# Mixers of three token blocks first, then all feed-forwards, their up projection as seven block products for eight

## What is computed

```python
def trunk(x, ...):
    y, c, g = mixer(rmsnorm(x, norm1[l]), ...)   # w_in, short conv and gated linear attention, w_out
    x = x + y
    y, f = conv_ffn(rmsnorm(x, norm2[l]), ffn_s[l], w_up[l], ffn_conv_w[l], w_down[l])
    x = x + y
    return rmsnorm(x, final_norm), ...

def conv_ffn(xn, prev, w_up, conv_w, w_down):
    u = xn @ w_up                          # 1024 -> 2 * 2816
    uc, new = causal_dwconv(u, prev, conv_w)   # three taps along the tokens
    a, g = jnp.split(uc, 2, axis=-1)
    return (jax.nn.silu(g) * a) @ w_down, new
```

## Time and profile before

| | us |
|---|---|
| median of 3 runs | 2595.28 |
| the profiled execution, from first to last instruction | 2592.0 |
| PE busy | 2487.6 (96%) |
| DVE busy | 1388.8 (54%) |
| ACT busy | 861.8 (33%) |
| POOL busy | 646.4 (25%) |

### The profile page before, as it was taken

How to read it: one execution, slowest core, us unless ns; L and a number is a source line. 1 busy time by engine, 2 the same in 40 slices (tenths; PEclk the granted TensorE clock), 3 DMA queues, 4 the chain that set the end, 5 groups by cost and what they waited for, 6 DMA issues and landing times.

```text
span 2592.0 us, 34435 instructions
## 1 busy us (share of the span) xinstructions
PE 2487.6 (96%) x12744; PEld 2159.8 (83%) x12744; DVE 1388.8 (54%) x2125; ACT 861.8 (33%) x1807; POOL 646.4 (25%) x364
## 2 busy tenths in 40 slices
PE   7999999999999999999999999999999999999996
PEld 7878777788888888887998998798888898898895
DVE  3025556555555555556303446576666666666667
ACT  4332332423332332224622233162332332332333
POOL 2211113233223322223112111322222222222220
PEclk9999999999999999999999999999999999999998
DMA  4111131211111111112411012111111111111101
GB/s 154 58 35 33 35 102 41 74 49 41 49 49 49 42 40 48 49 49 65 151 33 41 25 33 96 35 43 48 40 33 47 40 33 48 40 32 49 40 24 71
DMA packets 154669, 133.77 MB, mean 52 GB/s; under 512 B 5325, under 2 KB 137762, under 8 KB 154594
## 3 DMA queue, kind: packets, MB, share of 16 engines
q1 hardware_dynamic: 154593, 132.72, 16.3%
HBM read 123.69 MB, written 9.01 MB: 51 GB/s over the span
## 4 chain that ended last, share of the span: by engine, by line
PE 72%; issue 12%; DVE 9%; POOL 4%; ACT 3%; DVEq 0%; DMA 0%; ACTq 0%; POOLq 0%; SPq 0%
PE ps L989 23%; PE ps L991 22%; PE ps L990 22%; POOL w_lo L425 3%; DVE resid L1485 3%; POOL hid_lo L668 1%; PE ps L1016 1%; DVE up_a L1502 1%; DVE conv_y L1406 1%; PE ps L1081 1%; DVE x_n L1268 1%; PE ps L1098 1%; PE ps L1102 1%; PE ps L1105 1%; DVE conv_y L1437 1%
## 5 line engine op out<-in xcount | busy, mean ns | idle before, releaser
L989 PE MATMUL ps<-xt_hi,w_hi 128*128 128x512 f32 (+5 forms) x2688 | 947.3, 352 | 8.3 <-DVE xt_lo L1276 7.1
L991 PE MATMUL ps<-xt_lo,w_hi 128*128 128x512 f32 (+5 forms) x2688 | 938.4, 349 | 0.0
L990 PE MATMUL ps<-xt_hi,w_lo 128*128 128x512 f32 (+5 forms) x2688 | 938.3, 349 | 0.0
L425 POOL TENSOR_TENSOR w_lo<-raw,w_hi 128x1024 fp32r<-128x1024 f32 x196 | 489.5, 2504 | 1086.6 <-ACT w_hi L420 1086.6
L989 PEld LDWEIGHTS ps<-xt_hi,w_hi 128*128 128x128 f32 x2688 | 513.7, 191 | 62.7 <-issue 14.1
L990 PEld LDWEIGHTS ps<-xt_hi,w_lo 128*128 128x128 f32 x2688 | 513.8, 191 | 46.9 <-issue 0.2
L991 PEld LDWEIGHTS ps<-xt_lo,w_hi 128*128 128x128 f32 x2688 | 514.4, 191 | 43.2
L1485 DVE TENSOR_TENSOR resid<-resid,ps 128x512 f32<-128x512 f32 x748 | 467.1, 680 | 1.3
L938 ACT ACTIVATE up_u<-ps 128x512 f32<-128x512 f32 (+2 forms) x220 | 112.7, 512 | 666.9 <-PE ps L991 656.0
L989 PE MATMUL ps<-w_hi,hid_hi 128*128 128x512 f32 x704 | 281.8, 400 | 47.0 <-DVE resid L1485 46.1
L991 PE MATMUL ps<-w_lo,hid_hi 128*128 128x512 f32 x704 | 279.8, 397 | 0.0
(11 more groups left out here) (155 smaller groups left out, 2088.5 us busy)
## 6 DMA issues: line engine op xcount, KB each, us to landing
raw<-in_w_up_dram SPq DMA_DIRECT2D x88, 512.0 KB, 3.8
raw<-in_w_in_dram SPq DMA_DIRECT2D x48, 512.0 KB, 3.7
raw<-in_w_down_dram SPq DMA_DIRECT2D x44, 512.0 KB, 4.7
x_in<-in_x_prompt_dram SPq DMA_DIRECT2D x32, 512.0 KB, 4.3
raw<-in_w_out_dram SPq DMA_DIRECT2D x16, 512.0 KB, 3.7
out_dram<-x_n SPq DMA_DIRECT2D x16, 512.0 KB, 2.6
...
```

The costliest lines, as they stand in the source:

```text
L425: pool.tensor_tensor(w_lo[:, s, :], raw[:, s, :], w_hi[:, s, :].bitcast(F32), ALU.subtract).then_inc(lo_ready[s], 1)
L989: pe.matmul(out, lh, rh, start=(first and n == 0), stop=False)
L990: pe.matmul(out, ll, rh, start=False, stop=False)
L991: last = pe.matmul(out, lh, rl, start=False, stop=end)
```

## The change

The token blocks are three: 768, 768, and 512 with the 64 of the running stream (580 columns). First the mixers of all three run, one after the other. Each ends with its second RMSNorm, whose normalised activations are kept as plain fp32 (`xs`); VectorE forms four sums of their quarters (`combine`, halves of the 1024 rows by halves of the columns), and seven operands are stored to DRAM (`x_ops`), as is the residual (`x_mid`). Then the feed-forwards of the three blocks run.

The up projection of a step is now a 2 by 2 by 2 block product in Strassen's manner (Winograd's form): the two halves of the contraction, gate and value half of the weights, and two halves of the token columns (`HALF`, 384 or 290). `up_product` computes seven products of 12 matmuls in place of eight. Its operands are kept in SBUF for a whole block (`xo`, high and low parts); those of the weights are made anew in each step: VectorE sums (`sum_up`, four of 128x512), ScalarE high parts (`high_up`, seven of 128x512), GpSimd low parts (`low_up`, seven of 128x512). VectorE puts the four output quarters together (`r_2`, `r_3`, `put`), and taps, SiLU, product and high and low part of the hidden tile are done once over the whole block of 768 or 578 columns, after the seventh product. The down products of tile f - 2 (`tail`) and f - 1 (`head`) stand between the seven products. The last RMSNorm of a block is done inside steps 0 and 1 of the next one.

The down products, the number of down additions for a token tile and the work of the mixer stages on a token are those of before; weights of the mixer are loaded and split three times in place of two.

The diff, cut to its core:

```diff
-BT = SEQ // 2
-GAP = 2
-NCOL = [BT, BT + GAP + DEC]
-TILES = [BT // P, BT // P + 1]
-CHUNKS = [[(0, 512), (512, 512)], [(0, 364), (364, 364), (728, 362)]]
+NB = 3
+T0 = [0, 768, 1536]
+BTS = [768, 768, 512]
+GAP = 2
+TILES = [6, 6, 5]
+NCOL = [768, 768, 580]
+HALF = [384, 384, 290]
+CHUNKS = [[(0, h), (h, h)] for h in HALF]
+TAIL_SHARE = {12: [2, 2], 10: [2, 1]}
+HEAD_SHARE = {12: [1, 2, 2, 2, 1], 10: [1, 2, 2, 1, 1]}
...
+        x_mid = nc.dram_tensor("x_mid", [SEQ + DEC, D], F32).ap()
+        x_ops = nc.dram_tensor("x_ops", [NB, NP, P, 4, CMAX], F32).ap()
...
     @block.sync
...
+            def load_x_op(b, i):
+                c = HALF[b]
+                sp.dma_start(xo_raw[:, i, 1, :].rearrange("p (k c) -> p k c", k=4)[:, :, 0:c],
+                             x_ops[b, i, :, :, 0:c]).then_inc(xo_loaded[i], 16)
...
+                n2.wait(sp, "hi", 2 * nt)
+                for i, k, c0 in ((0, 0, 0), (2, 4, 0), (6, 4, c)):
+                    sp.dma_start(x_ops[b, i, :, :, 0:c], xs[:, k:k + 4, c0:c0 + c]).then_inc(ops_stored, 16)
+                sp.wait_ge(x_sums, sums_before(b + 1))
+                for i, n in X_SUM.items():
+                    sp.dma_start(x_ops[b, i, :, :, 0:c], tst[:, n, :, 0:c]).then_inc(sums_stored, 16)
...
+                    for t in range(4) if f == 0 else range(4, TILES[b - 1]):
+                        store_result(b - 1, t)
+                        if t < TILES[b]:
+                            load_resid(b, t)
+                if isinstance(f, int) and f == NF - 1 and b + 1 < NB:
+                    for i in range(NP):
+                        sp.wait_ge(up_done, NP * g + i + 1)
+                        load_x_op(b + 1, i)
+                if more:
...
     @block.gpsimd
...
+            def ffn_step(b, f, par, more=True):
+                g = b * NF + f
+                low_up(g, NP - 1)
+                prev = before(b, f, 1)
+                if prev:
+                    pool.wait_ge(h_hi, g)
...
+                                       ALU.subtract).then_inc(h_lo, 1)
+                if isinstance(f, int) and f == 0 and b:
+                    low_x(b, 6)
+                for i in range(NP - 1):
+                    if more:
+                        low_up(g + 1, i)
+                    if i == 1:
+                        pool.wait_ge(wd_high, g + 1)
+                        pool.tensor_tensor(wd_lo[:, par, :], wd_raw[:, :], wd_hi[:, par, :].bitcast(F32), ALU.subtract).then_inc(wd_low, 1)
+                    if isinstance(f, int) and f == NF - 1 and b + 1 < NB and i - 1 in LOW_BY_P:
+                        low_x(b + 1, i - 1)
...
     @block.scalar
...
+            def finish_up(b, f):
+                g = b * NF + f
+                w = tap_cols(b)
+                act.wait_ge(taps_g, 2 * (g + 1))
+                act.activation(up_y[:, 1, 0:w], up_y[:, 1, 0:w], ACT.Silu).then_inc(silu, 1)
+                act.wait_ge(c12_read, g + 1)
+                keep_rows(b, f)
+                wait(act, h_lo, g)
+                taps_start(b, 0, f).then_inc(y_a, 1)
...
+            def ffn_step(b, f, par, more=True):
+                g = b * NF + f
+                h = HALF[b]
+                edge = f if isinstance(f, int) else None
+                prev = before(b, f, 1)
+                if prev:
+                    finish_up(*prev)
+                act.wait_ge(up_done, NP * g + 1)
+                wait(act, c21_read, g)
+                act.activation(r_1[:, 0:h], ps[:, 3 * par, 0:h], ACT.Copy).then_inc(r1_read, 1)
+                act.wait_ge(wu_summed, 4 * g + 4)
+                high_up(g, 6)
+                if edge == 0 and b:
+                    high_x(b, 4)
+                if prev:
+                    high_hidden(*prev, 1 - par)
+                if edge == 0 and b:
+                    high_x(b, 5)
+                    high_x(b, 6)
+                if more:
+                    act.wait_ge(wu_loaded, 32 * (g + 2))
+                    high_up(g + 1, 0)
+                    act.wait_ge(up_done, NP * g + 2)
+                    act.wait_ge(wu_summed, 4 * (g + 1) + S2 + 1)
+                    high_up(g + 1, 1)
+                act.wait_ge(wd_loaded, 16 * (g + 1))
+                if prev:
+                    wait(act, down_done, down_before(*prev))
+                act.activation(wd_hi[:, par, :], wd_raw[:, :], ACT.Copy).then_inc(wd_high, 1)
+                act.wait_ge(up_done, NP * g + 3)
+                wait(act, taps_a, 2 * g)
...
+                wait(act, taps_g, 2 * g)
+                earlier_rows(b, 1, f)
+                act.wait_ge(c21_read, g + 1)
+                wait(act, gated, g)
+                taps_start(b, 1, f).then_inc(y_g, 1)
+                if more:
+                    act.wait_ge(up_done, NP * g + 6)
+                    high_up(g + 1, 5)
+                if edge == NF - 1 and b + 1 < NB:
+                    high_x(b + 1, 2)
+                    high_x(b + 1, 3)
+                if edge in (0, 1) and b:
+                    act.preload_act_table_set("natural_log_exp_and_others")
+                    for t in range(4) if edge == 0 else range(4, TILES[b - 1]):
+                        final_rstd(b - 1, t)
...
     @block.tensor
...
-                            columns(m, (par * 2 * nch + slot) % 4, c0, n).then_inc(ffn.up_done, 1)
-                            if not first_f:
-                                down(f - 1, 1 - par, pair + (par - 1), down_share(b, slot))
+            def up_product(b, par, i):
+                c = HALF[b]
+                bank = {0: 3 * par, 2: 3 * par, 4: 2, 6: 2}.get(i, 1)
+                return product(ps[:, bank, 0:c], [
+                    (wq_hi[:, i, k * P:(k + 1) * P], wq_lo[:, i, k * P:(k + 1) * P],
+                     xo[:, i, 0, k * c_of(k):k * c_of(k) + c], xo[:, i, 1, k * c_of(k):k * c_of(k) + c]) for k in range(4)],
+                    first=i in (0, 1, 4), skip=True)
...
+                    if i == 0:
+                        wait(pe, c11_read, g - 1)
+                    if i == 1:
+                        wait(pe, c21_read, g)
+                    if i == 2:
+                        pe.wait_ge(r1_read, g + 1)
+                    if i == 3:
+                        pe.wait_ge(r2_read, g + 1)
+                    if i == 4:
+                        wait(pe, c12_read, g)
+                    if i == 5:
+                        pe.wait_ge(r3_read, g + 1)
+                    if i == 6:
+                        pe.wait_ge(c22_read, g + 1)
+                    up_product(b, par, i).then_inc(up_done, 1)
+                    if i < 2 and prev2:
+                        down(*prev2, par, tails[i])
+                    if i == 2 and prev:
+                        down_ready(*prev)
+                    if i >= 2 and prev:
+                        down(*prev, 1 - par, heads[i - 2])
...
     @block.vector
...
+                def combine(c0, w):
+                    h = HALF[b]
+                    a, bb = xs[:, 0:4, c0:c0 + w], xs[:, 4:8, c0:c0 + w]
+                    c, d = xs[:, 0:4, h + c0:h + c0 + w], xs[:, 4:8, h + c0:h + c0 + w]
+                    t1, t2, t3, n4 = (tst[:, n, :, c0:c0 + w] for n in range(4))
+                    dve.tensor_tensor(t1, c, a, ALU.subtract).then_inc(x_sums, 1)
+                    dve.tensor_tensor(t3, d, c, ALU.subtract).then_inc(x_sums, 1)
+                    dve.wait_ge(x_sums, done + 1)
+                    dve.tensor_tensor(t2, d, t1, ALU.subtract).then_inc(x_sums, 1)
+                    dve.wait_ge(x_sums, done + 3)
+                    dve.tensor_tensor(n4, bb, t2, ALU.subtract).then_inc(x_sums, 1)
+                    return done + 4
...
+            def sum_up(g):
+                a0, a1, g0, g1 = (wu_raw[:, n, :] for n in range(4))
+                s1, s2, s3, s4 = (wu_sum[:, n, :] for n in range(4))
+                dve.wait_ge(wu_loaded, 32 * (g + 1))
+                wait(dve, wu_lo, NP * g)
+                dve.tensor_tensor(s1, g0, g1, ALU.add).then_inc(wu_summed, 1)
+                dve.wait_ge(wu_summed, 4 * g + 1)
+                dve.tensor_tensor(s2, s1, a0, ALU.subtract).then_inc(wu_summed, 1)
+                dve.tensor_tensor(s3, a0, g0, ALU.subtract).then_inc(wu_summed, 1)
+                dve.wait_ge(wu_summed, 4 * g + 2)
+                dve.tensor_tensor(s4, a1, s2, ALU.subtract).then_inc(wu_summed, 1)
...
+                tail(0)
+                dve.wait_ge(up_done, NP * g + 2)
+                dve.wait_ge(r1_read, g + 1)
+                dve.tensor_tensor(r_2[:, 0:h], ps[:, 1, 0:h], r_1[:, 0:h], ALU.add).then_inc(r2_read, 1)
+                tail(1)
+                if edge == 0 and b:
+                    low_x(b, 5)
+                if more:
+                    sum_up(g + 1)
+                if edge == 1:
+                    dve.wait_ge(resid_ready[0], 16 * 4 * (b + 1))
+                head(2)
+                dve.wait_ge(up_done, NP * g + 4)
```

(26 more changed lines are left out.)

1697 lines of the change are left out of this document (908 added, 789 removed).

## The result

The changed kernel takes 2706.24 us (median of 4 runs, 2705.39 to 2707.3); the kernel before, on the same chip, 2594.57 (2593.25 to 2595.38). The ratio is 1.0432 with a 95% interval of 1.0419 to 1.0445: **4.3% slower**.

The account below looks back on a forecast made before the run. Before: one feed-forward bound by PE, the other also by late VectorE; after: PE waiting for the hidden tile. 1042 + 14 + 1601 + 46 + 31 = 2734, plus 3.3: 2737 us; own range 2690 to 2790, 8 in 10 2550 to 2850.

Parts of the forecast that it names:

- 43 large periods: Steps of the 768-token blocks: period 24.8 us plus 0.5 for the clock, 25.3 each, 1088 together.
- 22 small periods: Steps of the small block: 21.8 us with PE idle 3.9, plus 1.5 for the clock, 23.3 each, 513 together.
- two changes of block: Between feed-forward blocks, operand loads and splits and the last norm hold up ScalarE's SiLU: 23 us each, twice 46.
- PE's own work: Large feed-forward step: 84 matmuls of 384 columns at 0.177 us and 36 of 512 at 0.233, 23.3 us.
- The chain: Large step, sixth product issued to hidden tile's low part: 14.95 us, GpSimd delaying two taps; with PE's 9.86, period 24.8.
- The clock in large blocks: PE waits 1.5 us a period; the clock falls in a third of the steps, 0.5 us a step.
- First step: Start of the feed-forwards: operands pass ScalarE, VectorE and GpSimd at some 2.4 us each, 14.4 for six.
- Mixers: Up to the first up product: 980 now, 5 for narrower chunks, 38 mixer changes, 29 feed-forward start, less 10: 1042 us.
- weights late: Rival, feed-forward steps: single-buffered wu_raw loads come two us late in every step, 2867 us; chance 0.06.
- GpSimd falls into the gaps: Rival, feed-forward steps: both GpSimd subtractions run while VectorE waits for ScalarE, PE never waits, 2554 us; chance 0.25.
- one of the two only: Rival: only one of GpSimd's two subtractions avoids the taps; steps 24.0 and 21.8 us, 2650 us; chance 0.12.
- VectorE becomes the bound: Rival, feed-forward steps: nine VectorE operations each wait 1 us for GpSimd, 27.5 us a large step, 2869 us; chance 0.12.

Follow-up runs that it names:

- the first two runs: Changed kernel with GpSimd's low part of operand 6 moved behind the hidden tile's: 2630.77 us; additionally operand 5's low part made by VectorE: 2602.24 us.
- the run with `r_2` first: Changed kernel with both collisions out, more PE cover for the hidden tile, and r_2 added ahead of the first two down additions on VectorE: 2575.28 us.

## Why the prediction was right, and where it was off

The sign, the mechanism and the place were right, and the time was 31 us too high (2737 against 2706.24), within its own range of 2690 to 2790. Term by term, with the cuts that the prediction had: its first step ends, and its end begins, when PE has issued a sixth product (1053.51 in the first step, 2670.87 in the last).

| term | predicted | measured |
|---|---|---|
| to the first up product | 1042 | 1021.8 |
| first step, to the sixth product issued | 14.4 | 31.7 |
| 43 large periods | 1088 (25.3) | 1037 (24.1) |
| 22 small periods | 513 (23.3) | 525 (23.9) |
| two changes of block (measured: all that steps have over the periods above) | 46 | 55 |
| end | 31 | 33.7 |

The errors partly cancel: mixers 20 and large periods 51 too high, first step 17, small periods 12, changes 9 and end 3 too low. So the total is nearer than its terms, and that is luck.

- **PE's own work** (23.3 us): too high by 0.5. The floor is 22.8. 384 columns take 0.173 us from start to start (twelve from 1304.53 to 1306.61), not the interpolated 0.177, and 512 columns 0.228, not 0.233. By the formula of the Trainium skill that was weighed there ("TensorE: Matmul & The Clock Gate", Back-to-back issue gap) 84 x 0.1625 + 36 x 0.2158 would be 21.4, an estimate; the measured floor is nearer to the interpolation. The page gives that formula for a matmul in isolation and has it too high for a stream of 512 columns; here the stream is slower than the formula, 228 ns against 216.
- **The chain** (14.95 us, period 24.8): right in every link of the large block, 0.8 us too long. With the clock's 0.5 on top the forecast had 25.3 for a measured 24.1. The forecast let a tap wait for GpSimd's whole 1.2 us, it waited 0.8: GpSimd's row begins at 1302.86, while the first tap still runs.
- **The clock in large blocks** (0.5 a step): did not fall at all. With a floor of 22.8 PE loses 1.3 us in each step, and at that the clock held 1.00. In the small block it is idle 3.2 us and the clock fell in every step: 2.1 us, not 1.5.
- **First step** (14.4): 31.7, so 17 us too low, the largest error for its size. I counted six operands at 2.4 us and left out that the result quarters share the same engines: PE waits 3.56 us for ScalarE's `r_1`, which stands behind seven copies of 1.5 us, and 9.37 for VectorE's `r_3`:

```profile
1049.76 0.66 PE L1163 MATMUL ps<-xo,wq_hi 128*128 128x384 f32 x1 [9.37 <-DVE r L1811]
```

  `r_3` stands on VectorE behind the four sums for the next step, and these waited 11.61 us for the load of `wu_raw`. With its one buffer that load is issued only at 1039.57, when GpSimd is through the low parts of this step, which stand between low parts of 3.5 us of the activation operands. The rival "weights late" was right in this one place.
- **Mixers**: 20 us too high. The three joints have 68 us of idle time (21.7, 23.9, 22.6) where 60.5 and 6.5 for the clock were counted, so their sum was right, though the share of the clock was not: the run that kept PE awake there gained nothing. The rest was in the mixers' bodies. PE is busy 925.9 us where it was 935.3 (450.25 + 485.01 in the earlier trace rows): 9 less, not 5 more. Its idle time outside the joints is 28, where 44.5 stood in the two mixers: 17 less, not 10.
- **Changes of block** (46): measured 55, and the forecast had them as one row of ScalarE's work. In the run with `r_2` first they are 64; leaving out the norms there, on which the 23 us each rested, gives 10, leaving out the operands 25.
- A count that bore no price: a third load of the mixer's weights is 32 blocks (96 low parts on `L417` in three mixers), not 36.

**The rivals.** "GpSimd falls into the gaps" and "one of the two only" did not happen, but the first two runs made them: 2602 and 2631 us, where 2554 and 2650 had been worked out. The first was too low mainly because 18.9 was taken for a small step that is 21.0 (46 us); the large step, put 0.5 too high, and the mixers made up for the low first step and changes of block. "VectorE becomes the bound" is refuted by the run without its sums. "Weights late": PE itself waited 4.7 us in all for a low part of a weight, and the late load cost it 9.4 more in the first step by way of `r_3`; in steady steps there was no such wait.
